# Expert items of 128 and 192 rows in turns, expert 0 first, its weights loaded early, and a last combination without GpSimd

## The reference

```
top_v, top_i = lax.top_k(logits, TOP_K)
gates = jax.nn.softmax(top_v, axis=-1)
...
for e in range(N_EXPERTS):
    out = out + comb[:, e:e + 1] * swiglu(t, wg[e], wu[e], wd[e])
```

## Time and profile before

| | us |
|---|---|
| median of three runs | 1494.28 |
| the profiled execution's own time | 1497.01 |
| its span | 1495.2 |
| TensorE busy (matmul) | 1307.3 |
| VectorE busy | 962.7 |
| ScalarE busy | 668.6 |
| GpSimd busy | 127.4 |

### The profile page before, as it was taken

How to read it: one execution, slowest core, us unless ns; L and a number is a source line. 1 busy time by engine, 2 the same in 40 slices (tenths; PEclk the granted TensorE clock), 3 DMA queues, 4 the chain that set the end, 5 groups by cost and what they waited for, 6 DMA issues and landing times.

```text
span 1495.2 us, 16139 instructions
## 1 busy us (share of the span) xinstructions
PE 1307.3 (87%) x5853; PEld 1036.6 (69%) x5853; DVE 962.7 (64%) x1264; ACT 668.6 (45%) x834; POOL 127.4 (9%) x147
## 2 busy tenths in 40 slices
PE   1888989799999999997979984599999999999990
PEld 1775447688887888876854572488888887788770
DVE  5866781665466456567575335467676788888885
ACT  4434431622122122234445330355556476677762
POOL 1270060000000000003200002000000000000004
PEclk9998989899999999998999996699999999999995
DMA  9930332145464456434700002966758699999964
GB/s 341 323 113 30 139 120 78 43 145 193 141 211 149 156 175 236 144 136 117 303 1 0 1 1 95 325 203 226 257 184 274 205 343 350 349 385 359 347 247 182
DMA packets 141361, 285.08 MB, mean 191 GB/s; under 512 B 6926, under 2 KB 48444, under 8 KB 141308
## 3 DMA queue, kind: packets, MB, share of 16 engines
q1 hardware_dynamic: 131116, 250.29, 48.4%
q0 software_dynamic: 10048, 34.08, 6.2%
q10 hardware_dynamic: 144, 0.00, 0.0%
HBM read 264.69 MB, written 19.66 MB: 190 GB/s over the span
## 4 chain that ended last, share of the span: by engine, by line
PE 76%; DVE 12%; ACT 5%; issue 4%; DMA 2%; POOL 1%; POOLq 0%; SPq 0%; ACTq 0%; DVEq 0%
PE ps L566 19%; PE ps L568 18%; PE ps L567 18%; PE ps L578 3%; PE ps L919 3%; PE ps L920 3%; DVE acc L1392 3%; ACT spl L1243 2%; PE ps L728 2%; PE ps L747 2%; PE ps L707 2%; DVE spl L1782 1%; DVE xfull L1792 1%; PE ps L716 1%; DMA x<-in_x 1%
## 5 line engine op out<-in xcount | busy, mean ns | idle before, releaser
L1782 DVE TENSOR_TENSOR spl<-mraw,spl 128x2048 fp32r<-128x2048 f32 (+1 forms) x146 | 308.4, 2115 | 112.6 <-ACT spl L1243 112.0
L1243 ACT ACTIVATE spl<-mraw 128x2048 fp32r<-128x2048 f32 (+1 forms) x146 | 257.9, 1775 | 155.9 <-PE ps L920 75.5
L1049 ACT ACTIVATE spl<-raw 128x2048 fp32r<-128x2048 f32 (+2 forms) x56 | 100.7, 1799 | 233.0 <-PE ps L568 193.2
L566 PE MATMUL ps<-hT,spl 128*128 128x512 f32 x416 | 165.5, 398 | 7.8 <-DVE hT L1453 7.8
L1376 DVE TENSOR_TENSOR spl<-raw,spl 128x2048 fp32r<-128x2048 f32 (+2 forms) x56 | 120.8, 2158 | 76.2 <-ACT spl L1049 75.6
L567 PE MATMUL ps<-hT,spl 128*128 128x512 f32 x416 | 164.1, 395 | 0.0
L568 PE MATMUL ps<-hT,spl 128*128 128x512 f32 x416 | 163.9, 394 | 0.0
L566 PE MATMUL ps<-spl,xgT 128*128 128x512 f32 (+1 forms) x384 | 145.8, 380 | 7.7 <-DVE xgT L1800 4.0
L568 PE MATMUL ps<-spl,xgT 128*128 128x512 f32 (+1 forms) x384 | 143.6, 374 | 0.0
L567 PE MATMUL ps<-spl,xgT 128*128 128x512 f32 (+1 forms) x384 | 143.5, 374 | 0.0
L1392 DVE SCALAR_TENSOR_TENSOR acc<-raw,cond,acc 128x512 f32<-128x512 f32 x154 | 118.7, 771 | 5.4
(11 more groups left out here) (315 smaller groups left out, 2307.9 us busy)
## 6 DMA issues: line engine op xcount, KB each, us to landing
raw<-in_w_mod SPq DMA_DIRECT2D x48, 1024.0 KB, 6.3
mraw<-in_moe_w_down SPq DMA_DIRECT2D x40, 1024.0 KB, 5.9
mraw<-in_moe_w_gate SPq DMA_DIRECT2D x34, 1024.0 KB, 5.5
mraw<-in_moe_w_up SPq DMA_DIRECT2D x32, 1024.0 KB, 6.9
mraw<-in_moe_w_gate SPq DMA_DIRECT2D x16, 768.0 KB, 6.2
mraw<-in_moe_w_up SPq DMA_DIRECT2D x16, 768.0 KB, 6.8
raw<-in_ffn_w_gate SPq DMA_DIRECT2D x11, 1024.0 KB, 8.2
raw<-in_ffn_w_up SPq DMA_DIRECT2D x11, 1024.0 KB, 5.4
```

The source lines that it names most:

```text
L566: mm(o, lh, rh, start=start, stop=False)
L1049: A(spl[:, s % SPLS, 0, 0:n], raw[:, r % RAWS, 0:n], ACT.Copy).then_inc(hi_ready, 1)
L1243: A(spl[:, (SB + j) % SPLS, 0, 0:w], mraw[:, j % MRAWS, 0:w], ACT.Copy).then_inc(hi_ready, 1)
L1782: V.tensor_tensor(o[:, 1, 0:w], mraw[:, j % MRAWS, 0:w], o[:, 0, 0:w].bitcast(F32), ALU.subtract).then_inc(lo_ready, 1)
```

## The change

The items take turns: one loop does a small and a large item per round, and a second loop the small items that are left. The number of items is at least 2 `n2` + 1, so that every large item has a small one before it and one more follows; items without rows would fill up. `n4` = 2 `n2` is where the second loop begins. The table has two rows, one for the small and one for the large items. Expert 0's rows are cut into small items only, and as it is first of the small ones it leads. Thresholds that differ by expert stand in `thr`, which GpSimd fills.

Since the first item's expert is known, SP loads its first four units as soon as their raw buffers are free in the mixing part of layer 1, and ScalarE and VectorE split the first two before the update after the out projection. SP no longer waits for the scatters before it issues expert weights. A small item turns and splits the half tile of the next large item too; a large item turns only the whole tile. The first item's rows are a whole tile alone. ScalarE and VectorE load the counts after the first item's rows instead of before. In the last combination VectorE does all: the weighted sum, its product with the gain, and one operation that scales by the inverse root and adds to `x`.

Cut to its core:

```diff
-MORE_THAN = (0, P, P + HP, 2 * P + HP, 3 * P)
 ROWS2 = P + HP
+MORE_THAN = ((0, P + HP, 3 * P, NEVER), (P, 2 * P + HP))
+MORE_THAN_0 = ((-1, P, 2 * P, 3 * P), (NEVER, NEVER))
+SCRATCH_TILES = 19
...
+        def counts(eng):
+            n = eng.value_load(eti[0:1, 0:1], min_val=3, max_val=MAXI)
+            n2 = eng.value_load(eti[0:1, 1:2], min_val=1, max_val=MAX2)
+            return n, n2, eng.value_load(eti[0:1, 2:3], min_val=2, max_val=2 * MAX2)
...
 SP
-            eng.wait_ge(lo_ready, SB)
-            eng.wait_ge(lg_ps, 1)
-            eng.wait_ge(tab_ready, 1)
-            eng.wait_ge(scat_dma, 16 * 2 * T)
...
+                if i is None:
+                    eng.wait_ge(lo_ready, SB - RAWS + j + 1)
+                else:
+                    eng.wait_ge(lo_ready, i * EU + (SB + j - MRAWS + 1))
...
+            for j in range(RAWS):
+                unit(None, 0, j)
+            eng.wait_ge(lg_ps, 1)
+            eng.wait_ge(tab_ready, 1)
+            n, n2, n4 = counts(eng)
+            with eng.Fori(0, n2) as i:
+                e = expert(i + n2 + 3)
+                for j in range(RAWS, EU):
+                    unit(i * 2, e, j)
+                e = expert(i + (3 + MAXT))
+                for j in range(EU):
+                    unit(i * 2 + 1, e, j)
+                e = expert(i + n2 + 4)
+                for j in range(RAWS):
+                    unit(i * 2 + 2, e, j)
+            with eng.Fori(n4, n) as k:
...
 GpSimd
+            eng.wait_ge(x_upd, T * (2 * L - 2) + 1)
+            for r in range(6):
+                w = divmod(r, 4)
+                g.memset(thr[:, r, 1:E], float(MORE_THAN[w[0]][w[1]]))
+                ins = g.memset(thr[:, r, 0:1], float(MORE_THAN_0[w[0]][w[1]]))
+            ins.then_inc(thr_ready, 1)
...
-            for t in range(T - 1):
-                eng.wait_ge(scaled, t + 1)
-                g.tensor_tensor(x[:, t, :], x[:, t, :], ym[:, t, :], ALU.add).then_inc(x_final, 1)
...
 TensorE, ScalarE, VectorE
-                with eng.Fori(0, n2) as i:
-                    item(i, 2)
-                with eng.Fori(n2, n) as i:
-                    item(i, 1)
+                with eng.Fori(0, n2) as i:
+                    item(i * 2, None, i)
+                    item(i * 2 + 1, i, None)
+                with eng.Fori(n4, n) as k:
+                    item(k, None, None)
...
 ScalarE, before the update of layer 1's mixing part
+                    for j in range(2):
+                        eng.wait_ge(mraw_full[j], 16)
+                        eng.wait_ge(w_used, SB + j - SPLS + 1)
+                        A(spl[:, (SB + j) % SPLS, 0, :], mraw[:, j, :], ACT.Copy).then_inc(hi_ready, 1)
...
 ScalarE and VectorE, at j == 16
-                            for b in range(tiles):
-                                rows(b, i + 2)
+                            rows(0, i + 2)
+                            if next_pair is not None:
+                                rows(1, next_pair + 1)
...
 VectorE, routing
-                for r, rows_before in enumerate(MORE_THAN):
-                    ins = V.tensor_scalar(above[:, r, :], cnt[:], float(rows_before), None, ALU.is_gt)
+                eng.wait_ge(thr_ready, 1)
+                link(V.tensor_tensor(above[:], cnt[:].unsqueeze(1).to_broadcast([P, 6, E]), thr[:], ALU.is_gt))
...
 VectorE, last combination
+                        after(V.scalar_tensor_tensor(out=ym[:, t, :], in0=yg[:, t, 1, :], scalar=gt[:, 1, t:t + 1],
+                                                     in1=ym[:, t, :], op0=ALU.mult, op1=ALU.add), ym_ready, t + 1)
+                        V.tensor_tensor(yg[:, t, 1, :], ym[:, t, :], gp[:, 2, :], ALU.mult).then_inc(scaled, 1)
...
-                        V.scalar_tensor_tensor(out=ym[:, u, :], in0=ym[:, u, :], scalar=rinv[:, u:u + 1],
-                                               in1=gp[:, 2, :], op0=ALU.mult, op1=ALU.mult).then_inc(scaled, 1)
+                        V.scalar_tensor_tensor(out=x[:, u, :], in0=yg[:, u, 1, :], scalar=rinv[:, u:u + 1],
+                                               in1=x[:, u, :], op0=ALU.mult, op1=ALU.add).then_inc(x_final, 1)
```

More of the change, by code:

```diff
@@ L187, in build @@
         msk = little("msk", [P, T + 1, E])
+        thr = little("thr", [P, 6, E])
         gpos = little("gpos", [P, T, E])
@@ L194, in build @@
         cnt = little("cnt", [P, E])
-        above = little("above", [P, len(MORE_THAN), E])
+        above = little("above", [P, 6, E])
         pairs = little("pairs", [P, 2, E])
@@ L518, in _ @@
             eng.wait_ge(tab_ready, 1)
[L519 to L520 removed]
+            n, n2, n4 = counts(eng)
             eng.sem_inc(ye_free, 1)
[L522 to L529 removed]
+            g.dma_start(xg[0][:], tiles_dram[bass.ds(n2 * ROWS2, P), :]).then_inc(xg_dma[0], 16)
@@ L920, in mm2, with item @@
                 return mm(o, both, wl, start=False, stop=stop)
-            def item(i, tiles):
+            def item(i, h, next_pair):
+                tiles = 1 if h is None else 2
+                count = (i, h)
                 def product(b, o, whole, half, k, weight, start, stop):
@@ L1630, in mixer @@
                         lo(W_FF + i)
+                else:
+                    for j in range(2):
+                        eng.wait_ge(hi_ready, SB + j + 1)
+                        o = spl[:, (SB + j) % SPLS]
+                        V.tensor_tensor(o[:, 1, :], mraw[:, j, :], o[:, 0, :].bitcast(F32), ALU.subtract).then_inc(
+                            lo_ready, 1)
             def dense():
@@ L1855, in item @@
                         if j == 16:
-                            for b in range(tiles):
-                                rows(b, i + 2)
+                            rows(0, i + 2)
+                            if next_pair is not None:
+                                rows(1, next_pair + 1, i + 2)
                     if tiles == 2:
-                        eng.wait_ge(ye_low, i + 1)
+                        eng.wait_ge(ye_low, h + 1)
                         o = ye[1][0:HP, :].rearrange("p (h c) -> p h c", h=2)
                         V.tensor_tensor(o, ps[0:HP, 6:8, :], o, ALU.add).then_inc(ye_ev[1], 1)
-                part(0, 0)
                 rows(0, 1)
-                part(0, 1)
-                rows(1, 1)
+                n, n2, n4 = counts(eng)
                 with eng.Fori(0, n2) as i:
-                    item(i, 2)
-                with eng.Fori(n2, n) as i:
-                    item(i, 1)
+                    item(i * 2, None, i)
+                    item(i * 2 + 1, i, None)
+                with eng.Fori(n4, n) as k:
+                    item(k, None, None)
                 for t in range(T + 1):
```

173 lines of the change are left out of this document (80 added, 93 removed).

## The result

| | before | after |
|---|---|---|
| median (lowest to highest), five runs each, same chip | 1494.07 (1490.26 to 1497.96) | 1510.25 (1506.12 to 1514.94) |
| span of the profiled execution | 1495.2 | 1508.7 |
| ratio, 95% interval | | 1.0117, 1.0098 to 1.0135 |

The change costs 16 us. The forecast was 1501.5, slower, with a range that ended at 1508; the time lies 2 us above it. The sign was right and the size less than half of it.

The account below looks back on a forecast made before the run. The prediction took TensorE to fill large items and VectorE to be late at small items' ends. Stage +12.1, start -0.5 and last combination -4.3 made +7.3, carried to a median of 1501.5; range 1488 to 1508.

Parts of the forecast that it names:

- Small before large: Three small items in the expert stage prepare the next large item's half rows, delaying VectorE 4.1 us each: +12.4.
- Large before small: Expert stage: a small item after a large one stalls 0.91 at its third unit; 1.1 each, two more: +2.2.
- half turns: Large items no longer do eight short turns on TensorE, saving 0.65 us each, three times: -2.0.
- First item: Start of the expert stage: the first item no longer waits for half rows at the half clock: -0.5.
- The scatters: Start of the stage: weight units 4 to 7 share the DMA engines, leaving GpSimd's scatters a 0.66 share: +4.0.
- starved scatters: Rival, start of the stage: GpSimd's queue gets a third, last scatter about 9.5 us late; 1506; chance 0.15.
- Fetch: Start of the stage: the fetch of `xg` meets fewer weights and no half rows beside it: -4.5.
- third count: Start of the stage: GpSimd has one more count to load: +0.5.
- routing: Table on VectorE before the stage: five comparisons become one and one chained addition goes: -0.5.
- Early splits: Expert 0's first two units, split under the out projection, cost nothing; 1.9 if the second came late.
- Last combination: End of the kernel: VectorE does everything without GpSimd's additions beside it: -4.3, bounds 0 and 5.5.
- The transfers did not pace the small items: Small items don't wait for weight transfers; the rival that they do had 15 us gained, 1487, chance 0.08.

Follow-up runs that it names:

- the run with that work alone: Kernel before, its five small items of the second loop also turning, scaling and splitting 64 rows nobody reads: 1511.80 against 1493.04, ratio 1.0118.
- the run with the rows first: Changed kernel with SP issuing the first item's unit 4 and following only after its first rows have landed: 1504.61 against 1495.12, ratio 1.0055.
- the three edits: Changed kernel with SP's unit 4 after the first rows, a Silu ahead of the loop, half rows split after the next item's first unit: 1493.68 against 1493.04.
- the run with the half rows two units later: Changed kernel with the next large item's half rows split after that item's first unit, on ScalarE and VectorE: 1502.52 against 1495.12, ratio 1.0063.
- the one with the combination alone: Kernel before with only the new last combination, all additions on VectorE: 1487.97 against 1495.12, ratio 0.9958.

## Why the prediction was wrong, point by point

- *Small before large, +12.4.* Right: 11.06 and 12.86 us on VectorE as read from the large item, +4.1 a small item in the run with that work alone.
- *Large before small, +2.2, and half turns, -2.0.* Their sizes were right: without table loads a small item is 56.16 where the sum had 51.0 + 4.1 + 1.1 = 56.2, and a large one at full clock 80.26 where it had 80.3.
- **The small item's head, in the step "large before small": failed.** The sum moved a small item to the head of the first loop and asked only for the stall of 0.91; the wait there was 2.28. That two table loads stand in every round of that loop, in the large items, where nothing waits for ScalarE, could be read in the trace of before. They cost 3.0 and 2.8: 5.8 of the 7.1 us by which the stage was missed. Half of it is the later third unit, half the clock that fell behind the longer wait.
- **The clock: not a term of the sum.** Idle time of "some 4.8 in all" was forecast for TensorE at a small item's end (it was 2.84 and 2.06), at the full clock throughout. Besides its share in the table loads the half clock cost 0.3 and 2.0 where it ran into the first and second large item (80.6 and 82.3 against 80.3).
- *First item.* By the same terms the first small item comes to 57.7 (51.0, 4.1, and the 3.1 of a first item less 0.5); it took 56.8, table loads and all. Its half clock at the start ended sooner: twelve products took 4.3 us (954.64 to 958.94), in the kernel before about 5.2. Why it ended sooner stays open. With it the stage's miss is made up: 5.8 for the table loads, 2.3 for the clock in the large items, -0.9 here, 7.2 against 7.1.
- **The scatters, +4.0: mis-sized, +6.9.** The mechanism was right (the run with the rows first takes it away whole); the share of 0.66 came from a stretch with another mix and was 47% here, after 1.5 us with hardly any. The rival, *starved scatters*, named the point from which it decides, less than half of the bytes; that is where it came out, at +6.9. Its own +9.5 doesn't follow from its terms: with a third of 373 GB/s until the 4.2 MB of weights are in, the last scatter comes some 11 late.
- *Fetch -4.5 with a third count +0.5, routing -0.5.* Right: -4.2 together from the landing of the scatters to that of the rows, and -0.5.
- *Early splits at no cost.* Right: ScalarE's two copies stand at 868.51 and 879.39, the sum of squares at 882.05 after 0.74 of idle time.
- *Last combination, -4.3.* Right in kind, -5.3.
- *The transfers did not pace the small items.* Right: no copy waited for `mraw`, and alternating gained nothing.
- *The absolute times* "last scatter about 941" and "first product between 952 and 958" came true (941.0 and 954.6) by luck: the program was 2.4 us early at the sum of squares, which hid the scatters' miss.
- *The chances* had "the same" at 0.46 ahead of slower at 0.43. By the forecast's own measure of 0.5% the result, 1.0098 to 1.0135, is slower.

In all +7.1 in the stage, +2.6 at the start, -1.0 at the end: 8.7 above the +7.3 forecast. The upper end of the range had been drawn for the scatters alone, with no term for anything else that a small item could meet at its new place. The best version of all that ran is the old order with the new combination, 0.9958 of before.

## What to carry to other kernels

When an item moves to another place in a program, read what the old occupant of that place had in front of it: table loads, evictions and half rows are free in a long item and are paid in full in one that is already late. Take a queue's share from the same mix of transfers that will meet, and where only another mix is in the trace, let the range reach to the lesser share. When an engine is relieved, look at once for the term just below it: the three edits gained 6.4, 6.5 and 9.4 us one by one, 22.3, and 16.9 together. And when an edit that should help shows no gain, follow the engines' lines through the item: the turns that held the clock up gained 1.6 us in one place and lost it in the next.

## What the runs showed of the hardware

- TensorE fell to the half clock, in a stage in which it is busy over nine tenths of the time, behind waits of 2.3 us: after 1148.28 and after 1099.94 in the changed kernel. It isn't a matter of one wait's length: before, the wait of 1.80 ahead of the turns at 1241.78 had none behind it, the like with 1.90 at 1128.08 above had, and in the run with the half rows two units later none of them had, nor had its wait of 2.28 at 1093.58. What decides between these stays open; no run was made for it.
- The half clock costs nothing while TensorE waits for another engine anyway: 55.11 with it and 55.09 without. Behind the third unit of a small item, where no such wait follows for 26 us, it cost 1.6.
- Table loads depend on how a loop is entered. One Silu ahead of the loop took two loads out of every round.
- The time from the start of the program to the sum of squares differed between kernels that do the same up to there by up to 7.5 us (877.5 in the one with the combination alone, 885.0 in the one with the half rows in small items). TensorE's busy time up to there is 791.5 and 795.5 us, so some 4 of it are longer products; I did not follow the rest. Differences of the span below that can only be read from a common point onwards.
